# A two-block float32 transformer kernel: the rows of its split input get a pitch of 4352 B in place of 4160 B, and a table of row selectors is replaced by a broadcast identity column

## What is computed

```
def odd_mixer(h, w_in, dw_w, dw_b, ln_g, ln_b, w_out):
    proj = h @ w_in
    a, b, gate = jnp.split(proj, [CONV_WIDTH, 2 * CONV_WIDTH], axis=-1)
    glu = a * jax.nn.sigmoid(b)
    conv = lax.conv_general_dilated(
        glu, dw_w.astype(glu.dtype), window_strides=(1,), padding=[(CONV_K - 1, 0)],
        dimension_numbers=('NWC', 'WIO', 'NWC'), feature_group_count=CONV_WIDTH)
...
    meta = jnp.broadcast_to(meta_tokens.astype(x.dtype)[None], (B, N_META, D_MODEL))
    h = jnp.concatenate([meta, x], axis=1)
...
        proj = jnp.einsum('bld,de->ble', xn, w_in[layer])
...
        a = jnp.square(jax.nn.relu(jnp.einsum('bld,df->blf', hn, w_ff1[layer])))
        h = h + jnp.einsum('blf,fd->bld', a, w_ff2[layer])
```

## Time and profile before

| | us |
|---|---|
| median of 3 runs | 2044.05 |
| lowest and highest | 2043.05, 2047.81 |
| profiled execution, its own time | 2043.77 |
| span of its trace, first to last instruction | 2042.0 |
| TensorE (PE) busy | 1959.3 |
| VectorE (DVE) busy | 1301.3 |
| GpSimd (POOL) busy | 1143.0 |
| ScalarE (ACT) busy | 725.5 |

### The profile page before, as it was taken

How to read it: one execution, slowest core, us unless ns; L and a number is a source line. 1 busy time by engine, 2 the same in 40 slices (tenths; PEclk the granted TensorE clock), 3 DMA queues, 4 the chain that set the end, 5 groups by cost and what they waited for, 6 DMA issues and landing times.

```text
span 2042.0 us, 24981 instructions
## 1 busy us (share of the span) xinstructions
PE 1959.3 (96%) x9212; PEld 1563.4 (77%) x9212; DVE 1301.3 (64%) x1852; ACT 725.5 (36%) x1209; POOL 1143.0 (56%) x938
## 2 busy tenths in 40 slices
PE   7999999999998999899999799999999999999997
PEld 6887877778776788777887465687788887888885
DVE  6127653679997997351573477467544446777778
ACT  3002553342245452330120445324223224545542
POOL 4222115469988996435541200027867778988885
PEclk9999999999999999999999899999999999999999
DMA  5432116546554554437523543245567668666652
GB/s 191 136 113 82 42 42 241 176 167 192 178 165 146 184 175 156 155 134 247 186 70 103 115 100 74 114 155 167 196 209 238 198 219 311 222 252 215 217 186 104
DMA packets 104504, 335.43 MB, mean 164 GB/s; under 512 B 12672, under 2 KB 12928, under 8 KB 103616
## 3 DMA queue, kind: packets, MB, share of 16 engines
q1 hardware_dynamic: 55616, 192.74, 29.1%
q0 software_dynamic: 30384, 106.44, 15.6%
q10 hardware_dynamic: 18384, 34.66, 4.6%
HBM read 272.75 MB, written 46.20 MB: 156 GB/s over the span
## 4 chain that ended last, share of the span: by engine, by line
issue 33%; POOL 31%; PE 30%; DVE 3%; DMA 2%; ACT 1%; POOLq 0%; ACTq 0%; DVEq 0%
PE PS L1217 16%; PE PS L1762 13%; POOL WL L985 12%; POOL VSL L1172 3%; POOL RBM L1024 3%; POOL WL L1167 2%; POOL SQH L1024 2%; POOL WH L978 2%; DMA WH<-weights 1%; POOL VS L1156 1%; POOL VS L1164 1%; POOL VS L1159 1%; POOL WL L1174 1%; POOL WH L1142 1%; DVE ACC L3276 1%
## 5 line engine op out<-in xcount | busy, mean ns | idle before, releaser
L1217 PE MATMUL PS<-XHM,WH 128*128 128x512 f32 (+1 forms) x1464 | 527.0, 384 | 25.1 <-POOL WL L985 10.1
L1217 PE MATMUL PS<-XLM,WH 128*128 128x512 f32 (+1 forms) x1464 | 516.2, 377 | 0.0
L1217 PE MATMUL PS<-XHM,WL 128*128 128x512 f32 (+1 forms) x1464 | 513.9, 375 | 0.0
L978 POOL DMA_DIRECT2D WH<-weights x149 | 86.0, 577 | 721.5 <-PE PS L1217 706.8
L985 POOL TENSOR_TENSOR WL<-WRAW,WH 128x1024 fp32r<-128x1024 f32 x149 | 362.1, 2430 | 24.7 <-DMA WH<-weights 21.6
L1217 PEld LDWEIGHTS PS<-XHM,WH 128*128 128x128 f32 x1464 | 270.9, 190 | 90.5 <-POOL WL L985 15.9
L1217 PEld LDWEIGHTS PS<-XLM,WH 128*128 128x128 f32 x1464 | 277.3, 189 | 54.9 <-issue 1.7
L1217 PEld LDWEIGHTS PS<-XHM,WL 128*128 128x128 f32 x1464 | 277.3, 189 | 52.4
L2715 DVE SCALAR_TENSOR_TENSOR PS<-G,TAPW,PS 128x512 f32<-128x512 f32 x319 | 215.8, 749 | 0.6
L3276 DVE TENSOR_TENSOR ACC<-ACC,PS 128x1024 f32<-128x1024 f32 (+1 forms) x113 | 119.8, 1073 | 15.7 <-PE PS L1217 12.9
L1217 PE MATMUL PS<-OPH,VSH 128*128 128x512 f32 x256 | 99.9, 390 | 2.0 <-issue 1.7
(11 more groups left out here) (383 smaller groups left out, 3977.4 us busy)
## 6 DMA issues: line engine op xcount, KB each, us to landing
WRAW<-weights SPq DMA_DIRECT2D x211, 512.0 KB, 3.5
WH<-weights POOLq DMA_DIRECT2D x195, 512.0 KB, 4.6
OPR<-inner SPq DMA_DIRECT2D x56, 512.0 KB, 6.6
inner<-STAGE ACTq DMA_DIRECT2D x56, 256.0 KB, 4.6
inner<-TOUT ACTq DMA_DIRECT2D x48, 256.0 KB, 4.7
XTOK<-x SPq DMA_DIRECT2D x8, 512.0 KB, 7.3
x_kept<-X SPq DMA_DIRECT2D x4, 1024.0 KB, 7.1
X<-x_kept SPq DMA_DIRECT2D x8, 512.0 KB, 5.0
```

Source lines behind the costliest of these rows:

```text
L978: g.dma_start(WH[:, u, :], weights[WORDER[p]]).then_inc(w_hi[u], 16)
L1217: m = nc.tensor.matmul(dst[:, a:b], w, v[:, a:b], start=first and n == 0, stop=last and n == 2)
```

## The change

The pitch of the rows of `XHM` and `XLM` becomes 4 x 1088 = 4352 B, which is 17 x 256. The data stand at the end of each row (`[:, :, ROW - L:]`), so that the rows of `XH` and `XL` begin 256 B behind the rows of the buffer: all sixteen at 128 modulo 256. The two buffers grow by 8 x 192 B each, 3072 B in all. `ROWSEL` (4096 B) goes. All else that follows moves by multiples of 256 B (3072 up, behind `ROWSEL` 1024 down). The 528 columns are now cut at 272, so that the second piece starts with the same token as a multiple of 256 B: 272 + 256 in place of 264 + 264. The row selectors are read from the identity matrix: column b of its first 8 rows, read 128 times with a step of zero. `R11B` moves to the end part of `XLM`.

```
-MA = (META + HALF) // 2
+MA = META + HALF // 2
+ROW = 1088
...
-LA = LB = 264
+LA, LB = MA, HALF // 2
...
-        XHM = fixed("XHM", [P, KD, L], F32R)
-        XLM = fixed("XLM", [P, KD, L], F32R)
+        XHM = fixed("XHM", [P, KD, ROW], F32R)[:, :, ROW - L:]
+        XLM = fixed("XLM", [P, KD, ROW], F32R)[:, :, ROW - L:]
...
-        ROWSEL = fixed("ROWSEL", [8, 8, P])
...
-        R11B = at("R11B", [P, HALF], o_rowsel)
+        R11B = at("R11B", [P, HALF], o_xh + 65536)
...
+        def row_of(b):
+            return IDENT[0:8, b:b + 1].broadcast_to([8, P])
...
-            const(g.memset(ROWSEL[:], 0.0))
-            const(g.affine_select(out=ROWSEL[:], in_=ROWSEL[:], compare_op=ALU.not_equal, fill=1.0, base=0,
-                                  pattern=[[-1, 8], [0, P]], channel_multiplier=1))
...
-                pe.wait_ge(consts, 7)
+                pe.wait_ge(consts, 5)
...
-                    m = nc.tensor.matmul(bank(6, 2)[:, b * P:(b + 1) * P], ROWSEL[:, b, :], RR[:],
+                    m = nc.tensor.matmul(bank(6, 2)[:, b * P:(b + 1) * P], row_of(b), RR[:],
...
-                    m = nc.tensor.matmul(bank(4 + h)[:, b * P:(b + 1) * P], ROWSEL[:, b, :], RTH[h][:],
+                    m = nc.tensor.matmul(bank(4 + h)[:, b * P:(b + 1) * P], row_of(b), RTH[h][:],
...
-            act.wait_ge(consts, 9)
+            act.wait_ge(consts, 7)
...
-            dve.wait_ge(consts, 34)
+            dve.wait_ge(consts, 32)
```

More of the change, by code:

```diff
@@ L228, in build @@
         o_xh = top[0]
-        o_xl = o_xh + KD * L * 4
-        XHM = fixed("XHM", [P, KD, L], F32R)
-        XLM = fixed("XLM", [P, KD, L], F32R)
+        XHM = fixed("XHM", [P, KD, ROW], F32R)[:, :, ROW - L:]
+        XLM = fixed("XLM", [P, KD, ROW], F32R)[:, :, ROW - L:]
         XH, XL = XHM[:, :, META:], XLM[:, :, META:]
@@ L244, in build @@
         COLSEL = fixed("COLSEL", [P, 15])
-        o_rowsel = top[0]
-        ROWSEL = fixed("ROWSEL", [8, 8, P])
         GAINS = fixed("GAINS", [P, NGAIN, KD])
```

## The result

| | before | after |
|---|---|---|
| median of 6 runs of each, us | 2046.30 | 2035.86 |
| lowest and highest, us | 2043.05, 2048.88 | 2031.25, 2037.08 |
| profiled execution, its own time, us | 2043.77 | 2034.13 |
| span of its trace, us | 2042.0 | 2032.3 |

The ratio after to before is 0.9949, with a 95% interval of 0.9938 to 0.9960: 0.51% faster, 10.4 us by the medians and 9.6 us between the two profiled executions. The forecast was 14.7 us less, 2029.1; the time lies in the range (2020.5 to 2037.5) and on the forecast side, at 65 to 71% of the forecast size.

A forecast was written before the change was run, and what follows sets the result against it. PE's matmul stream was taken as the bound, with POOL and DVE nearly level in places. Gains by stretch, 7.2 + 1.0 + 1.5 + 0.2 + 2.9 + 1.9 = 14.7 us, took 2043.8 to 2029.1 us; range 2020.5 to 2037.5.

The forecast's parts named there:

- the neighbours: Rival: POOL and DVE also hold PE between 604 and 1125 us; 2032 to 2037.5 us, chance 0.16.
- medians of 389: Sign of being right: matmuls reading XHM and XLM show a median duration of 389 ns, where XHM had 393.
- 36 starts in 8.16 us: Sign of being right: the first projections run at the last phase's pace, 226.7 ns a matmul.
- The step: Start-to-start time of 512-column matmuls on XH and XL rows: 5.2 ns less for each.
- The rival by which the row start isn't the cause: XHM and XLM matmuls stay at 232 ns and the time at 2044 us; chance 0.08.
- The start: POOL's two instructions go, first weight DMAs issue earlier: 0 taken, ends a gain of 2.0 and a loss of 1.3 us.
- The cut: Short matmuls, 272 + 256 for 264 + 264: 2.5 ns saved a pair, ends 0 and 5 ns, 0 to 2.0 us.
- From 1003 to 1125 us: 549 matmuls, 236 of them short: gain of 1.6 us for the long and 0.3 for the short.
- From 795 to 1003 us: 869 matmuls, 196 of them short: four fifths of 3.5 us, 2.7, plus 0.2 for the short, 2.9 us.
- a mixed stream: CVH starts at 128 yet has median 393, explained by alternating CVL matmuls whose rows start elsewhere; no separate gain.
- The selector: 112 loads reading one element 128 times: taken as 0, with up to 21 us lost if twice as long and unhidden.
- the rival on the slow side: Reading one address repeatedly makes loads slow and DVE waits for each spread: 2071 us at three times the load; chance 0.04.

The follow-up runs named there:

- the first experiment: Changed kernel with the rows of XHM and XLM back at a pitch of 4160 B: 2046.65 us, ratio 1.0006 to the kernel before.
- the four places: Changed kernel, all XH and XL rows starting at 64, 0, 192 or 112 modulo 256 (four kernels): 2051.69, 2052.44, 2037.71, 2053.61 us.
- rows only: Changed kernel with columns cut 264 + 264 again and two idle POOL instructions ahead of its first weight DMA: 2027.81 us, ratio 0.9935 to the kernel before.
- the kernel with the wait: Changed kernel cut 264 + 264, POOL's first weight DMA waiting for the fifth block of input tokens: 2031.90 us, ratio 0.9937 to the kernel before.

## Why the prediction was right in direction and too large

**Where it fell.** The forecast's own bracket was 2026 to 2032 us with a chance of 0.66. The median, 2035.9, fell into the next one (2032 to 2037.5, chance 0.16), which was that of the neighbours. The mechanism that was forecast was there; what made the gain smaller was for the most part not the neighbours, but the terms told below. Of the signs named ahead, these came: medians of 389, 36 starts in 8.16 us, the convolution 6 us earlier, the loads (185 ns). These didn't: POOL and DVE stood no closer to full in the convolution (144.43 and 143.34 of 145 us), PE waited for `WL` not more often but longer (two waits, 4.2 us against 2.9), and the first product came at 22.40 us, not 20.9.

**The step was right in kind and a little too large.** 5.2 ns for each 512-column matmul was the forecast. The same 36 starts in 8.16 us came out exactly, but over the whole of the first 980 us it is 231.9 - 227.4 = 4.5 ns. The forecast took the best stretch of the last phase for all; over the 1386 matmuls ahead of 451 us that is 1.0 us too much. The rival by which the row start isn't the cause fell with the first experiment and the four places.

**Its reason was half right.** I named the row's own start at 128 modulo 256, as all the rows of the trace before allowed it: every stationary operand stood at 128 too, so that place and distance were the same thing. The kernels with moved weights told them apart. The sum doesn't suffer from it, by luck: the weights stood at 128. But whoever had carried "put rows at 128" to another kernel would have lost: the kernel with rows at 128 and weights at 192 is 14.5 us slower than the kernel before (1.5 of it at the start).

**The neighbours** held the gain where the forecast had them. With POOL at 5.46 us a job, 1.0 us was to be left between 451 and 604 us; "rows only" and the kernel with the wait have 1.2 each. In the changed kernel it is -0.3, with the half-clock time behind the second wait, which the sum didn't have. "Rows only" met one too, behind its first wait, and had 2.05 + 0.60 us of waiting against 2.08 + 2.09 here: the half-clock time of PE let POOL catch up. From 604 to 735 us 1.5 was forecast and 0.8 to 0.9 came.

**The start is the first term that failed.** The forecast took 0 from bounds of +2.0 and -1.3, with the sentence that what comes earlier only displaces what PE wants first. That sentence was right and its value was wrong: if it displaces the tokens, it costs. The lower bound, one weight chunk of the size of a block of tokens, was the mechanism itself, and 1.5 us was its price. The rows for it stood there: the issue, forecast at 8.6 us, falls well ahead of the last block of tokens, which is used at 14.70.

**The cut is the second.** It was taken as a saving of 2.5 ns a pair and costs 3 ns: over 408 pairs a loss of 1.2 us where a gain of up to 1.0 was taken. Both ends, 0 and 5 ns, rested on short matmuls that behave like long ones, by columns or by a fixed amount, with nothing lost at the distance 0. The starts say the opposite: at that distance 256 columns take 120.2 to 120.3 ns, elsewhere 116.0 to 118.3. Why, no run here shows. No row of a short matmul at either place stood behind the range, and so it should have reached to a loss.

**From 1003 to 1125 us** 1.9 us was forecast (1.6 for the long ones), and it was 0.1 to 0.3 in every trace with the new rows. PE leads there and its clock is full. Over 120 of its long matmuls, each weight block has three of 512 columns among six short ones. The timeline of PE in such a chunk, before:

```profile
1046.84 0.29 PE L1217 MATMUL PS<-XHM,WH 128*128 128x264 f32 x1
...
1053.95 0.28 PE L1217 MATMUL PS<-XHM,WH 128*128 128x264 f32 x1
```

And after:

```profile
1039.46 0.29 PE L1215 MATMUL PS<-XHM,WH 128*128 128x272 f32 x1
...
1046.60 0.29 PE L1215 MATMUL PS<-XHM,WH 128*128 128x272 f32 x1
```

Five blocks of nine matmuls lie between: 7.11 us before, 7.14 after. The long ones have the distance 0 and hardly get faster. By the starts of the kernel after, a 512-column matmul takes 227.3 ns when another long one follows, and when a short one does 233.1 (256 columns) and 232.2 (272); in the kernel before the same places took 231.5 on average, in "rows only" 232 to 234. The step that failed is that 5.2 ns were counted for every long matmul, whatever follows it; the rows that carried it, and the earlier trace rows, are both pure streams of long ones. The long ones here that are followed by a long one (some 180) went from 231.8 to 228.2 ns, 0.6 us in all, and the others and the short ones took most of that back.

**From 795 to 1003 us** 2.9 us was forecast, and 1.6 came after and 4.5 in "rows only". Of 670 long matmuls there only a few stand before a short one, so that this is another matter: at 4.5 ns each they would give 3.0. The clock is at its lower level for 6.8 us of this stretch in the trace before, for 10.2 after, and for 3.4 in the kernel with the wait, which gained 5.4; that fits. "Rows only" has 6.8 like the kernel before, and what gave it the other 1.5 us isn't shown.

`CVH`, which I explained as a mixed stream, fits the groups in the trace before: there too a row at 128 is slower than it could be while its neighbours stand elsewhere (230.0 ns against 226.7). But `CVL` was not moved, and so it isn't shown.

**The selector** costs nothing. The loads, before at 187 ns:

```profile
L1339 PEld LDWEIGHTS PS<-RT,IDENT x40: 180/185/185, 355.8 to 725.3; 8*128 8x128 f32 x40
```

Reading one element 128 times is no slower than reading 128, and the rival on the slow side falls.

**The account.** Rows alone 13.3 us by the ratio and 14.9 by the medians, where the sum without the terms of the short ones (0.2 + 0.3) was 14.2. Start and cut together take 0.14% back in the ratio, 2.9 us, of which 1.5 (start) and 1.2 (cut) are seen directly. The other terms were too large: by 1.5 us from 1003 to 1125, by 1.0 ahead of 451 (by the step), by 0.6 from 604 to 735. Without them the sum for the rows alone is 11.1 us; the interval (10.8 to 15.9) holds both 11.1 and 14.2, so that the runs can't tell them apart, and that the medians come out near 14.2 is luck as far as is known (the five runs lie between 2026.8 and 2032.9, and the places of lower clock move).

## What to carry to other kernels

Where a stream of long float32r matmuls sets the pace, compare the start-to-start time of its phases, and put moving and stationary operands at the same address modulo 256: here 4.5 ns of 232 each, over some 3,000 matmuls. Do it for all rows of a stream, since one row at the good distance among others stays slow. Change both sides in turn before you believe in an absolute place, and count the gain only for long matmuls among their like. An instruction taken out ahead of a DMA makes the DMA earlier: look what is still in flight at that time, and if it is wanted first, let the DMA wait for it.

## What the runs showed of the hardware that was not expected

- The pace of a stream of 512-column float32r matmuls depends on the distance of its two operands modulo 256: 227.4 ns at 0, 229.2 at +64, 232.8 at 128, 233.3 at -64, 236.1 at -16. It isn't symmetric, and being 16 B off is worse than being 64 B off. Rows at the distances +64, 128, -64 and 0 in turn give 231.9, where the four alone average 230.7; the ones at 0 take 230.0 among the others and 226.7 among themselves. What lies behind this stays open, and other distances were not run.
- At the distance 0 a matmul of 512 columns is 5 ns longer when a shorter one follows it (232 to 233 ns, against 227.3 when a long one does). At the other distances it isn't: 231.1 to 231.5 against 233.3 with the rows at 64, 231.5 against 231.9 in the kernel before. And one of 256 columns among short ones is slower at the distance 0 (120.2 to 120.3 ns) than at the others (116.0 to 118.3).
- 512 KB on one queue, started 2.27 us earlier, made 512 KB on another 1.3 us later for each chunk that ran beside it: the blocks' distance went from 1.28 to 2.55 us.
- A wait of PE that grew from 1.69 us to 2.05 us and more was followed by 3.4 us at the lower clock in six traces of six; in the seven traces whose longest wait in that stretch was 1.04 to 1.96 us the clock stayed full.
